# Index scores spread over nine in-projection tiles, five top-k tiles carried into the convolution

## What is computed

```
q, k, v, qi, ki, wi, z, xbc, dt_raw, ga, gs = jnp.split(h @ w_in, offsets, axis=-1)
dots  = einsum('bqhd,bsd->bqhs', qi, ki) * IDX_DIM ** -0.5          # index scores, 4 heads
score = einsum('bqh,bqhs->bqs', wi * IDX_HEADS ** -0.5, relu(dots))
score = where(kpos <= qpos, score, -inf)
_, idx = top_k(score, 256)                                          # keys each query may attend to
xbc   = silu(bias + sum_j xp[:, j:j + T] * w[j])                    # causal convolution, 4 taps
```

## Time and profile before

| | us |
|---|---|
| median of 3 runs | 3617.17 |
| lowest and highest run | 3615.83, 3621.35 |
| the profiled execution | 3622.78 |
| its span | 3621.0 |
| PE, DVE, ACT, POOL busy | 3482.4, 2015.4, 766.6, 1562.9 |
| mean granted TensorE clock | 0.968 of full |

### The profile page before, as it was taken

How to read it: one execution, slowest core, us unless ns; L and a number is a source line. 1 busy time by engine, 2 the same in 40 slices (tenths; PEclk the granted TensorE clock), 3 DMA queues, 4 the chain that set the end, 5 groups by cost and what they waited for, 6 DMA issues and landing times.

```text
span 3621.0 us, 56381 instructions
## 1 busy us (share of the span) xinstructions
PE 3482.4 (96%) x22350; PEld 3265.5 (90%) x22350; DVE 2015.4 (56%) x2956; ACT 766.6 (21%) x1539; POOL 1562.9 (43%) x675
## 2 busy tenths in 40 slices
PE   8999999998999999999789889999999999999998
PEld 7999999998986999999667747779999999999998
DVE  5333333346666999987756644775383534334334
ACT  2000000002232111233566424662110200000000
POOL 3533443432322444444337615994444243453351
PEclk9999999999998999999799977999999999999999
DMA  2111111112211222222263335863341111111111
GB/s 90 53 46 35 52 52 35 47 46 77 56 30 53 90 92 94 82 95 93 54 66 88 114 80 140 228 170 101 106 163 56 41 54 40 41 58 41 41 53 57
DMA packets 399840, 272.29 MB, mean 75 GB/s; under 512 B 61842, under 2 KB 375522, under 8 KB 399720
## 3 DMA queue, kind: packets, MB, share of 16 engines
q1 hardware_dynamic: 379896, 225.75, 23.2%
q10 hardware_dynamic: 19824, 44.95, 3.3%
HBM read 211.05 MB, written 59.81 MB: 75 GB/s over the span
## 4 chain that ended last, share of the span: by engine, by line
PE 89%; DVE 4%; issue 2%; POOL 2%; DMA 2%; ACT 1%; SPq 0%; another core or an unknown queue 0%; ACTq 0%; DVEq 0%; POOLq 0%
PE setA L365 10%; PE setA L366 10%; PE setB L365 10%; PE setB L366 10%; PE setA L367 10%; PE setB L367 10%; PE bankC L365 2%; PE bankC L367 2%; PE bankC L366 2%; PE bankD L367 2%; PE bankD L365 2%; PE bankD L366 2%; PE setB L517 1%; PE bankC L1497 1%; PE bankD L2074 1%
## 5 line engine op out<-in xcount | busy, mean ns | idle before, releaser
L345 POOL TENSOR_TENSOR whi<-wraw,ones 128x1024 fp32r<-128x1024 f32 x190 | 471.2, 2480 | 1639.4 <-PE setA L367 1034.4
L365 PE MATMUL setA<-hhi,whi 128*128 128x352 f32 (+1 forms) x2304 | 752.5, 327 | 21.1 <-POOL wlo L348 9.9
L365 PE MATMUL setB<-hhi,whi 128*128 128x352 f32 (+1 forms) x2304 | 747.2, 324 | 1.2 <-POOL wlo L348 1.2
L366 PE MATMUL setA<-hlo,whi 128*128 128x352 f32 (+1 forms) x2304 | 746.7, 324 | 0.0
L367 PE MATMUL setA<-hhi,wlo 128*128 128x352 f32 (+1 forms) x2304 | 745.7, 324 | 0.0
L366 PE MATMUL setB<-hlo,whi 128*128 128x352 f32 (+1 forms) x2304 | 742.3, 322 | 0.0
L367 PE MATMUL setB<-hhi,wlo 128*128 128x352 f32 (+1 forms) x2304 | 741.2, 322 | 0.0
L348 POOL TENSOR_TENSOR wlo<-wraw,whi 128x1024 fp32r<-128x1024 f32 x190 | 476.2, 2506 | 14.9
L365 PEld LDWEIGHTS setA<-hhi,whi 128*128 128x128 f32 x2304 | 437.2, 190 | 27.9 <-issue 18.8
L366 PEld LDWEIGHTS setA<-hlo,whi 128*128 128x128 f32 x2304 | 437.1, 190 | 1.7
L365 PEld LDWEIGHTS setB<-hhi,whi 128*128 128x128 f32 x2304 | 433.4, 188 | 5.3 <-issue 2.0
(11 more groups left out here) (415 smaller groups left out, 5516.6 us busy)
## 6 DMA issues: line engine op xcount, KB each, us to landing
wraw<-in_w_in SPq DMA_DIRECT2D x64, 512.0 KB, 3.8
wraw<-in_w_ffn_gate SPq DMA_DIRECT2D x44, 512.0 KB, 3.8
wraw<-in_w_ffn_up SPq DMA_DIRECT2D x44, 512.0 KB, 3.8
wraw<-in_w_ffn_down SPq DMA_DIRECT2D x44, 512.0 KB, 3.5
abc<-acsD SPq DMA_DIRECT2D x8, 2048.0 KB, 10.1
xcD<-cv ACTq DMA_DIRECT2D x24, 520.0 KB, 2.7
xc<-xcD SPq DMA_DIRECT2D x8, 1536.0 KB, 14.6
zD<-spill ACTq DMA_DIRECT2D x16, 524.0 KB, 2.7
```

The costliest lines, as they stand in the source:

```text
L345: pool.tensor_tensor(dst_cols(slot, hi), dst_cols(slot), ones[:, :].unsqueeze(1).to_broadcast([P, KD, P]), ALU.mult).then_inc(w_hi, 1)
L365: pe.matmul(out, w1, r1, start=start, stop=False)
L366: pe.matmul(out, w1, r2, start=False, stop=False)
```

## The change

The units of the index scores are taken head by head within a piece, and are put two by two after 26 of the 27 chunks of tiles 16 to 24. PE's and ACT's straight-line code is made longer for it (`SPILL2` = 10 tiles, 16 to 25), and POOL's masking is interleaved with its weight splits. The top-k keeps only query tiles 2 and 3 whole ahead of the convolution; tiles 4 to 8 leave their last 7, 8, 9, 10 and 11 rounds for the steps, one a step, and each writes its mask after its last round.

```diff
--- before.py
+++ after.py
@@ -732,9 +732,13 @@
                 [(qT, j) for j in range(KD)]
         NORM_UNITS = [(t, k, c) for t, k in HEADS[6:] for c in range(3)]
         NU = len(NORM_UNITS)
-        IDX_UNITS = [(t, h, o) for t in range(2, NT) for h in range(4) for o in range(0, WID[t], 512)]
+        IDX_UNITS = [(t, h, o) for t in range(2, NT) for o in range(0, WID[t], 512) for h in range(4)]
         IDX_END = {t: sum(u[0] <= t for u in IDX_UNITS) for t in range(1, NT)}
-        IDX_SLOT = [(0, IDX_END[3])] + [(IDX_END[t - 1], IDX_END[t]) for t in range(4, NT)]
+        IDX_TILES = (16, 25)
+        IDX_SLOT = [(min(s, len(IDX_UNITS)), min(s + 2, len(IDX_UNITS)))
+                    for s in range(0, 6 * (IDX_TILES[1] - IDX_TILES[0]), 2)]
+        assert IDX_SLOT[-1][1] == len(IDX_UNITS)
+        SPILL2 = 10
         QROWS = [P] * (NT - 1) + [LAST]
 
         def head_src(j):
@@ -839,8 +843,10 @@
             for j in range(2):
                 split_tile(pool, TILE_IN + 16 + j, raw_count(TILE_IN + 16), j, (gemm_done[j], 3 * (ORD_IN + 8)))
 
-            for j in range(2):
-                split_tile(pool, TILE_IN + 18 + j, raw_count(TILE_IN + 18), j, (gemm_done[j], 3 * (ORD_IN + 9)))
+            def split(j):
+                split_tile(pool, TILE_IN + j, raw_count(TILE_IN + j), j % 2, (gemm_done[j % 2], 3 * (ORD_IN + j // 2)))
+            for j in (18, 19):
+                split(j)
             pool.wait_ge(kit_stored, 32)
             pool.wait_ge(tok_evac, NT + 2)
             for t in range(2):
@@ -848,13 +854,21 @@
                 ch.run(pool.memset(m, 0.0))
                 ch.run(pool.affine_select(out=m, in_=m, compare_op=ALU.is_ge, fill=MASKED, base=t * P,
                                           pattern=[[-1, WID[t]]], channel_multiplier=1))
+            nxt = 20
             for t in range(2, NT):
+                last = next(s for s, (_, e) in enumerate(IDX_SLOT) if e >= IDX_END[t])
+                while nxt <= 16 + last // 3 + 2:
+                    split(nxt)
+                    nxt += 1
                 pool.wait_ge(idx_acc, IDX_END[t])
                 o, w = SOFF[t] + t * P, WID[t] - t * P
                 m = sc[0:QROWS[t], o:o + w]
                 pool.affine_select(out=m, in_=m, compare_op=ALU.is_ge, fill=MASKED, base=0,
                                    pattern=[[-1, w]], channel_multiplier=1).then_inc(sc_masked, 1)
-            pool_rest(pool, TILE_IN + 20, ORD_IN + 10, (N_IN - 20) // 2)
+            if nxt % 2:
+                split(nxt)
+                nxt += 1
+            pool_rest(pool, TILE_IN + nxt, ORD_IN + nxt // 2, (N_IN - nxt) // 2)
 
         def pool_rest(pool, n0, q0, pairs):
             with pool.Fori(0, pairs) as i:
@@ -906,15 +920,15 @@
                 u = 3 * (j - 6) + c - 1
                 if 0 <= u < NU:
                     head_squares(u)
-                if j >= 16:
+                if IDX_TILES[0] <= j < IDX_TILES[1]:
                     if (j, c) == (16, 0):
                         pe.wait_ge(tok_evac, NT + 2)
                     index_scores(3 * (j - 16) + c)
-            for j in range(2, 18):
+            for j in range(2, 16 + SPILL2):
                 gemm_tile(pe, TILE_IN + j, ORD_IN + j // 2, j % 2, between=functools.partial(beside, j))
-            with pe.Fori(0, (N_IN - 18) // 2) as i:
+            with pe.Fori(0, (N_IN - 16 - SPILL2) // 2) as i:
                 for j in range(2):
-                    gemm_tile(pe, i * 2 + (TILE_IN + 18 + j), i + (ORD_IN + 9), j)
+                    gemm_tile(pe, i * 2 + (TILE_IN + 16 + SPILL2 + j), i + (ORD_IN + 8 + SPILL2 // 2), j)
 
         def act_in(act):
             act_norm(act, 1)
@@ -984,20 +998,24 @@
                     qn, n = QROWS[t], min(512, WID[t] - o)
                     act.activation(relu[0:qn, u % 2, 0:n], CD[u % 2][0:qn, 0:n], ACT.Relu).then_inc(idx_relu, 1)
 
-            for j in range(2):
+            for m in range(SPILL2):
+                i, j = m // 2, m % 2
+                if i:
+                    act.wait_ge(slot_out[j], 16 * i)
                 for c, (o, w) in enumerate(CH):
-                    act.wait_ge(gemm_done[j], 3 * (ORD_IN + 8) + c + 1)
+                    act.wait_ge(gemm_done[j], 3 * (ORD_IN + 8 + i) + c + 1)
                     act.activation(spill2[:, j, o:o + w], SETS[j][:, c, 0:w], ACT.Silu).then_inc(gemm_evac[j], 1)
-                    if j == 0 and c == 0:
+                    if m == 0 and c == 0:
                         head_root(NU - 1)
-                    index_relu(3 * j + c)
-                act.wait_ge(gemm_evac[j], 3 * (ORD_IN + 9))
-                act.dma_start(zD[j * P:(j + 1) * P, :], spill2[:, j, :]).then_inc(slot_out[j], 16)
+                    if 3 * m + c < len(IDX_SLOT):
+                        index_relu(3 * m + c)
+                act.wait_ge(gemm_evac[j], 3 * (ORD_IN + 9 + i))
+                act.dma_start(zD[m * P:(m + 1) * P, :], spill2[:, j, :]).then_inc(slot_out[j], 16)
             act.wait_ge(idx_acc, len(IDX_UNITS))
 
             q = ORD_IN + 8
             for dst, pairs, func, m0 in ((zD, 8, ACT.Silu, 0), (gaD, 4, ACT.Sigmoid, 8), (gsD, 4, ACT.Sigmoid, 12)):
-                with act.Fori(1 if m0 == 0 else 0, pairs) as i:
+                with act.Fori(SPILL2 // 2 if m0 == 0 else 0, pairs) as i:
                     spill_tile_pair(act, dst, func, i + (q + m0), i + m0, i)
 
             q = ORD_IN + 24
@@ -1119,21 +1137,22 @@
                 qn, w = QROWS[t], WID[t]
                 if t == 3:
                     for j in range(2):
-                        v.wait_ge(slot_out[j], 16)
+                        v.wait_ge(slot_out[j], 16 * (SPILL2 // 2))
                 v.wait_ge(topk_step, 2 * n)
                 v.tensor_scalar(mb[0:qn, MOFF[t]:MOFF[t] + w], sc[0:qn, SOFF[t]:SOFF[t] + w], TAKEN * 0.5, MASKED,
                                 ALU.is_gt, ALU.mult).then_inc(mb_ready, 1)
             v.wait_ge(sc_masked, NT - 2)
 
-            LATE = (NT - 4, NT - 3, NT - 2)
+            LATE = tuple(range(4, NT))
             EARLY = [t for t in range(2, NT) if t not in LATE]
             CONV_STEPS = CONVD // P // 2 - 1
+            LAST_STEP = {t: CONV_STEPS - (LATE[-1] - t) for t in LATE}
             n = 0
             for t in EARLY:
                 n = rounds_of(t, rounds, n)
                 bias_of(t)
             for t in LATE:
-                n = rounds_of(t, rounds - CONV_STEPS, n)
+                n = rounds_of(t, rounds - LAST_STEP[t], n)
 
             def conv(b):
                 j = b % 2
@@ -1146,14 +1165,13 @@
                                                  ALU.mult, ALU.add)
                     ins.then_inc(conv_step if tap < 3 else conv_done, 1)
             for i in range(CONV_STEPS + 1):
-                if i:
-                    for t in LATE:
+                for t in LATE:
+                    if 1 <= i <= LAST_STEP[t]:
                         n = rounds_of(t, 1, n)
+                        if i == LAST_STEP[t]:
+                            bias_of(t)
                 for j in range(2):
                     conv(2 * i + j)
-                    if i == CONV_STEPS and j == 0:
-                        for t in LATE:
-                            bias_of(t)
             v.wait_ge(mb_ready, NT - 2)
             v.wait_ge(conv_done, 24)
 
```

## The result

| | before | changed |
|---|---|---|
| median, us (8 runs each) | 3619.85 | 3632.18 |
| ratio to before, 95% interval | | 1.0033 (1.0021 to 1.0044) |
| profiled execution, us (span) | 3622.78 (3621.0) | 3625.78 (3624.1) |

A forecast was written before the change was run, and what follows sets the result against it. PE was taken as the bound (busy 96%), with DVE holding it up next at tile 52. The terms 19.2 + 2.3 + 3 = 24.5 us took the median from 3617.17 to 3641.7; range 3632 to 3649, with rival B 3630 to 3655.

The forecast's parts named there:

- DVE's lateness decides, PE's gain is lost: At tile 52: PE arrives at 1505.1, stands 43.7 us for block 0, and starts 19.2 us later than before.
- Rival A: Index stretch and tile 52: PE's 24.5 us gain stands, 3592.7 if DVE is in time; chance 4%, for some result between.
- PE's price for a pair: Index stretch: 25 later pairs cost 34.5 us at 1.70 ns a column plus 5.0 us way in and out, together 39.5.
- The last mask: Between the last index unit and top-k: Relu, multiply-adds and a mask take 1.5 us, so top-k starts at 1192.4.
- Top-k ahead of block 0: DVE's rounds before the first convolution: 348.1 us instead of 376.3, so block 0 begins at 1540.5.
- the way to tile 52: From block 0 to PE's tile 52: taps 3.97 us, then SiLU, store and first copy 4.3 us; start at 1548.8.
- the restart: After PE's wait at tile 52: the clock has to come back, costing 2.3 us.
- The steps: Convolution stage, two tiles a step: DVE needs 23.2 us against PE's 22.96; 3 us lost in all.
- The dearer sum of 3674: Convolution steps under the skill's exclusion rule at its worst: taps wait for all four split operations, steps lose 35 us.
- Sum: Whole kernel: 19.2 + 2.3 + 3 = 24.5 us slower, median 3641.7 instead of 3617.17.
- B: Convolution steps: both blocks of each step disturbed, DVE's steps become the bound, 3651.7 us; chance 20%.
- C: Index stretch: the clock falls between the spread pairs, top-k starts 18 us later still, 3660 us; chance 5%.

The follow-up runs named there:

- spread_only: The changed kernel with index units spread as changed but top-k divided as in the kernel before; ratio to before 1.0106.
- mask_first: The changed kernel with POOL masking query tile 8 before it splits the weights of tile 26, not after; ratio to before 1.0018.
- topk_only: The kernel before with only the top-k of tiles 4 to 8 moved behind, index units still in six bursts; ratio to before 1.0002.
- early_rounds: mask_first with two top-k rounds of query tile 2 after each pair of units from the ninth on; 3590.67 us against 3620.77, ratio 0.9915.
- head_order: The changed kernel with units in the old order (for each head all pieces), still two by two; ratio to before 1.0075.
- the second traces: The kernel before and the changed kernel each run once more, unaltered, for a second trace; the changed kernel's traced run took 3629.57 us.
- four_per_chunk: mask_first with four units behind each of 13 chunks instead of two behind each of 26; 3596.25 us against 3620.77, ratio 0.9936.

## Why the prediction was right, and where its sizes were off

**DVE's lateness decides, PE's gain is lost: right.** PE stands 51.0 us at tile 52 for ACT's copy of block 2, behind DVE's block 0; 43.7 were forecast, as PE came 13.9 us earlier than forecast and the copy 6.6 us. spread_only and mask_first move block 0 by +29.4 and -4.7 us and the total by +26 and -5; topk_only, where DVE is in time, moves nothing; early_rounds turns the loss into a gain of 0.85%. Rival A has the mechanism that these kernels use, but the changed kernel is not in its case.

**PE's price for a pair: wrong.** The step was "20,288 x 1.70 ns = 34.5 us", a sum over units one after the other. Neighbours in the new order are different heads, whose 64 rows lie in different halves of the array, and they run together. The 25 later pairs cost 26 us (1054.65, when the second chunk began, to 1176.83, when the projection goes on behind the last pair, less 25 x 3.83), not 39.5. head_order shows it from the other side. PE therefore reached tile 52 at 1491.2, not 1505.1, and the scores ended earlier too. Two signs of this in the profile of before were overlooked:

```profile
1054.91 0.59 PE L894 MATMUL bankD<-ki,qiT 64*128 64x384 f32 x1 [1.00 <-ACT nrt L938]
1055.29 0.59 PE L894 MATMUL bankC<-ki,qiT 64*128 64x384 f32 x1
...
1099.53 1.12 PE L894 MATMUL bankC<-ki,qiT 64*128 64x512 f32 x2
...
1101.34 1.12 PE L894 MATMUL bankC<-ki,qiT 64*128 64x512 f32 x2
...
1112.52 1.12 PE L894 MATMUL bankC<-ki,qiT 64*128 64x512 f32 x2
```

A unit is recorded as two matmuls. The first of the unit in `bankC` (1055.29) stands between the two of the unit in `bankD` (1054.91 and the 1055.34 of the earlier trace rows); these are heads 1 and 2, in different halves. And in the bursts each pair starts 1.81 us after the one before, whether the second unit has 384 columns (1099.53 to 1101.34) or 512 (1110.71 to 1112.52). So that pace was the Relu's, and what two neighbours cost PE could not be read from it. The Trainium skill (TensorE: Matmul & The Clock Gate, section "The mechanism" on small matmuls) says that matmuls on different row groups of the array overlap, with starts some ns apart. The trace agrees, with starts 10 ns apart.

**The last mask: missed.** The 1.5 us between PE's last unit and the first round were 9.3 (1176.83 to 1186.09), 8.0 of them a wait for a mask behind a weight split in POOL's order. The diff showed that order, and the prediction put ACT's and POOL's moved instructions at nothing, looking only at whether they held up PE.

**Top-k ahead of block 0, the way to tile 52, the restart: right.** 347.8 us for 348.1; 1533.90 to 1542.25, 8.35 us, for 8.3; 2.4 us for 2.3.

**The steps: right, slightly dear.** 23.14 us a step for 23.2, with 12.0 us for the six taps of a step, for 7.91 + 3.97. The dearer sum of 3674 therefore did not come about. From tile 52 to the end of tile 71 (1775.4) PE took 233.2 us, 0.9 more than 20 tiles with the restart; 3 had been put down.

**Sum.** The two misses pull against each other, and that is luck: the last pair was over 14.1 us earlier than forecast, the way from there to the first round took 7.8 us more, and so the top-k began 6.3 us earlier (1186.09 for 1192.4). Tile 52 was 12.7 us later than before, for 19.2; the last block 15.8 us (19.0 between the second traces), for 24.5. Behind the last block the prediction had "the trace of before, 24 us later", and there the changed kernel is 9 to 13 us shorter in the traces, which leaves 3 us in the first pair of traces and 10 in the second. The measured 12 us are more than either, because both traced runs of the changed kernel (3625.78 and 3629.57 us) were below its median of 3632.18. Which mechanism shortens that part was not settled. Against the first trace of before, some 5 of the 11 us are there 110 us behind the last block, in a stretch where the profile puts waits of up to 8.6 us down to no engine of the core; but the two traces of before differ there by 3 us themselves. Another 3 to 4 us lie behind the attention. The kernels differ in their length of code and in when they get there, and no experiment here separated these.

The prediction's own range was added up to 3649; its parts (3, 2 and 4 us above 3641.7) give 3651.

**Rivals B and C.** B (the steps bind) did not come true: PE lost 0.9 us there. C (the clock falls in the spread) neither: the clock was 1.00, in four_per_chunk too, which had a wait for a Relu in nearly every group of four units.

## What to carry to other kernels

When an engine's idle time is taken away, ask which other engine's start hangs on the end of the spread work: here 26 small pieces in PE's gaps put off 348 us of DVE work by 47 us, and PE gave all of it back in one wait. Spread only as far as the consumer allows, or let the consumer begin on the part that is ready; the same spreading, with the last mask moved too, then gave 1.2% instead of costing 0.3%. And before a small matmul is priced by the pace of a burst, see whether that pace is its own or that of the engine that empties the bank.

## What the runs showed of the hardware

Two fp32 matmuls of 64 rows each, in different halves of the partitions and into different banks, ran together: a pair of 512 columns each took 1.06 us, and two of the same half 1.91 us, the second starting 0.96 us after the first. PE waits of up to 0.7 us, in nearly each of 13 groups of 24 projection matmuls and four units, left the granted clock at 1.00; over the window of the six bursts, with waits of up to 1.7 us, it was 0.78 to 0.80 in three traces. After 51 us without a matmul, 17 matmuls ran at half clock, against 16 behind the short waits before 1136.54 in the earlier trace rows. A DVE mask of 128x384 took 2.34 us beside a weight split on POOL and 0.36 without one, while the rounds' MAX8 of 128x1024 took 1.23 us with POOL's splits in the same stretch as without.
